# A hybrid decoder step: softmax steps, mixed norm and samples' output set in other slots

## The reference

```python
xn = rms_norm(x, norm1_g); proj = xn @ w_in                     # 2048 -> 5128 columns
y_pool, y_conv = causal_pool_mix(...), h_b * causal_dwconv(h_c * h_x, ...)   # 512 wide each
y_att = attn_fn(q, k, v, logf)                                  # 8 heads of 128
mix = concatenate([rms_norm(y_pool), rms_norm(y_conv), rms_norm(y_att)])     # 512, 512, 1024 wide
x = x + mix @ w_o
xn2 = rms_norm(x, norm2_g); a, gate = split(xn2 @ w_up, 2)
x = x + (silu(causal_dwconv(a, ...) + ffn_conv_b) * gate) @ w_down
```

## Time and profile before

| what | value |
|---|---|
| median of 3 runs | 2859.94 us (2858.17 to 2873.46) |
| the profiled execution, its own time | 2860.91 us |
| its span (first to last instruction) | 2859.3 us |
| PE busy | 2640.5 us, 92% |
| PE in the chain that ended last | 77% |
| DMA in that chain | 11% |
| slots 2 to 80 | about 100 to 611 us |
| mixers, heads | 611 to 716 us, 716 to 998 us |
| mixed norm up to chunk 2 of the output projection | 998 to 1050 us |
| output projection | up to 1276 us |
| second norm and first feed-forward tiles | 1276 to 1323 us |

### The profile page before, as it was taken

The page is one execution under the profiler, slowest core; times in us unless marked ns, Lnnn a source line. Parts: engine busy times, 40 slices in busy tenths (PEclk is TensorE's granted clock), DMA queues, the critical chain, the costliest instruction groups (busy, mean ns, idle before and its releaser), DMA issues.

```text
span 2859.3 us, 50522 instructions
## 1 busy us (share of the span) xinstructions
PE 2640.5 (92%) x19656; PEld 2322.7 (81%) x19656; DVE 1429.8 (50%) x5629; ACT 730.8 (26%) x979; POOL 149.5 (5%) x305
## 2 busy tenths in 40 slices
PE   5899999987677779989999999999999999999998
PEld 3799889862233246668999999999999999999998
DVE  4787766766788442235343443434343434343433
ACT  4332222222333241223222222222222222222221
POOL 0100000013111112100000000000000000000000
PEclk8999999989777789988999999999999999999999
DMA  7689999998999867724222322222222232222221
GB/s 240 243 286 339 324 338 333 337 341 314 391 384 366 323 238 261 250 94 148 89 89 95 101 100 90 89 89 89 89 89 89 95 101 100 89 89 89 89 89 64
DMA packets 274531, 532.94 MB, mean 186 GB/s; under 512 B 16410, under 2 KB 177787, under 8 KB 272980
## 3 DMA queue, kind: packets, MB, share of 16 engines
q1 hardware_dynamic: 216301, 367.81, 37.1%
q0 software_dynamic: 37744, 136.17, 12.9%
q10 hardware_dynamic: 20247, 25.73, 2.5%
HBM read 503.94 MB, written 24.05 MB: 185 GB/s over the span
## 4 chain that ended last, share of the span: by engine, by line
PE 77%; DMA 11%; DVE 6%; issue 2%; ACT 1%; SPq 1%; POOLq 0%; ACTq 0%; POOL 0%; DVEq 0%
PE ps L708 77%; DMA t_r<-in_cache_k 8%; DVE t_work L1786 4%; DMA t_r<-in_cache_v 2%; DMA t_wraw<-in_w_in 1%; PE ps L711 1%; ACT t_wh L1228 0%; DVE t_wl L1623 0%; SPq L582 0%; DMA t_wraw<-in_w_o 0%; DVE t_nmax L1924 0%; DVE t_work L1623 0%; SPq L568 0%; DVE t_auxL L1931 0%; DVE t_xl L1623 0%
## 5 line engine op out<-in xcount | busy, mean ns | idle before, releaser
L708 PE MATMUL ps<-t_xh,t_wh 128*128 128x260 f32 (+1 forms) x4352 | 950.1, 294 | 11.2 <-DVE t_xl L1623 11.1
L708 PE MATMUL ps<-t_xh,t_wl 128*128 128x260 f32 (+1 forms) x4352 | 937.3, 291 | 0.0
L708 PE MATMUL ps<-t_xl,t_wh 128*128 128x260 f32 (+1 forms) x4352 | 935.8, 291 | 0.0
L1623 DVE TENSOR_TENSOR t_wl<-t_wraw,t_wh 128x1024 fp32r<-128x1024 f32 x376 | 460.2, 1225 | 896.1 <-ACT t_wh L1228 896.0
L1228 ACT ACTIVATE t_wh<-t_wraw 128x1024 fp32r<-128x1024 f32 x376 | 398.0, 1060 | 1648.6 <-PE ps L708 1648.4
L708 PEld LDWEIGHTS ps<-t_xh,t_wh 128*128 128x128 f32 x4352 | 686.7, 190 | 86.7 <-issue 60.5
L708 PEld LDWEIGHTS ps<-t_xh,t_wl 128*128 128x128 f32 x4352 | 686.8, 190 | 11.8
L708 PEld LDWEIGHTS ps<-t_xl,t_wh 128*128 128x128 f32 x4352 | 686.2, 190 | 9.4
L1786 DVE CUSTOM_DVE_ANT_0 t_work<-t_r,t_work 128x128 f32<-128x128 f32 x2048 | 455.2, 288 | 130.7 <-DMA t_r<-in_cache_k 119.8
L708 PE MATMUL ps<-t_hh,t_wh 128*128 128x260 f32 x1408 | 285.7, 284 | 3.4 <-issue 3.4
L708 PE MATMUL ps<-t_hh,t_wl 128*128 128x260 f32 x1408 | 284.6, 284 | 0.0
(11 more groups left out here) (256 smaller groups left out, 1187.0 us busy)
## 6 DMA issues: line engine op xcount, KB each, us to landing
t_r<-in_cache_k SPq DMA_DIRECT2D x256, 512.0 KB, 7.7
t_r<-in_cache_v POOLq DMA_DIRECT2D x244, 512.0 KB, 6.6
t_wraw<-in_w_up SPq DMA_DIRECT2D x44, 2048.0 KB, 8.0
t_wraw<-in_w_in SPq DMA_DIRECT2D x22, 2048.0 KB, 9.4
t_wraw<-in_w_down SPq DMA_DIRECT2D x22, 2048.0 KB, 7.8
t_wraw<-in_w_o SPq DMA_DIRECT2D x11, 2048.0 KB, 8.7
scr_proj<-t_stg ACTq DMA_DIRECT2D x40, 256.0 KB, 4.9
t_aux<-scr_proj ACTq DMA_DIRECT2D x8, 768.0 KB, 17.4
```

The source lines that it names most:

```text
L708: return pe.matmul(out, lhsT, rhs, start=start, stop=stop)
L1623: return dve.tensor_tensor(out, in0, in1, op)
```

## The change

Four things are edited.

1. **The relay's distances.** PE's three steps move from `K_END` + 1, 2, 4 to + 2, 4, 7; DVE's from + 1, 2, 3, 4, 5 to + 1, 3, 5, 6, 8; ACT's exponentials from + 3 to + 5. The first value page may come at + 6 instead of + 4. The table `VALUES` has after it, in every slot from 22 to 172, one pair of pages less done than before; the last pair is in slot 173 (before: 172).
2. **Half of the mixed norm beside head 7.** The totals of groups 0 and 1, their rstd and tiles 0 to 7 stand in slots 142 to 147 (`EARLY` = 142) with the stages of head 7; totals go through bank 5 of PSUM one after the other. The samples' share of these groups (`sample_squares`, `sample_sums`) moves too, its Ln and Exp on ACT to slot 148.
3. **The output projection begins at slot 150** instead of 152, and there are 182 slots instead of 184. Group 2 and tiles 8 to 15 remain in slots 149 and 150, with the heads and rests of the first four weight chunks between them.
4. **`sample_out_attention(8)` and `(10)`** stand ahead of `norm(1)` instead of behind the first step of the first feed-forward tile.

```diff
     at = 0
     for r in range(DEC):
-        at = max(at, k_end[r] + 4)
+        at = max(at, k_end[r] + 6)
...
 KEYS, VALUES, K_END, V_END = page_slots()
-OUT0 = TAIL + 3
+EARLY = TAIL - HSTEP
+OUT0 = TAIL + 1
...
 V_LAST = {s: r for r, s in enumerate(V_END)}
-MISC = sorted({s + d for s in K_END for d in (1, 2, 4)} | {s + 1 for s in V_END})
+MISC = sorted({s + d for s in K_END for d in (2, 4, 7)} | {s + 1 for s in V_END})
...
+        TOTALS = (5, 5, 2)
...
@@ -874,14 +876,14 @@
                     return
                 if MISC_N[s] > 1:
                     pe.wait_ge(m_read, MISC_N[s] - 1)
-                if s - 1 in K_LAST:
-                    pe.wait_ge(c_mx, K_LAST[s - 1] + 1)
+                if s - 2 in K_LAST:
+                    pe.wait_ge(c_mx, K_LAST[s - 2] + 1)
                     last = tr(ps[0:HEADS, 7, 0:P], mx8[:, :], P)
-                if s - 2 in K_LAST:
-                    pe.wait_ge(c_dg, K_LAST[s - 2] + 1)
+                if s - 4 in K_LAST:
+                    pe.wait_ge(c_dg, K_LAST[s - 4] + 1)
                     last = mm(ps[:, 7, P:P + HEADS], ones[0:HEADS, :], diag[:, :])
-                if s - 4 in K_LAST:
-                    pe.wait_ge(c_ps, K_LAST[s - 4] + 1)
+                if s - 7 in K_LAST:
+                    pe.wait_ge(c_ps, K_LAST[s - 7] + 1)
                     last = mm(ps[:, 7, 136:144], ones[:, :], ps8[:, :])
...
-                    mm(ps[:, g, :], ones[:, :], msum[g]).then_inc(x_tot, 1)
+                    if g == 1:
+                        pe.wait_ge(x_log, 1)
+                    mm(ps[:, TOTALS[g], :], ones[:, :], msum[g]).then_inc(x_tot, 1)
...
+                if s in (EARLY, EARLY + 2):
+                    mix_totals(((s - EARLY) // 2,))
+                if s == EARLY + 4:
+                    pe.wait_ge(x_log, 2)
+                    pe.wait_ge(y_norm, Y_SQ)
+                    mm(ps[:, 5, 0:64], ones[:, :], sqS[:, 0:64]).then_inc(y_norm, 1)
                 if s == TAIL:
-                    mix_totals((0, 1))
-                    pe.wait_ge(y_norm, Y_SQ)
                     pe.wait_ge(h_rowsC, 2 * HEADS)
-                    mm(ps[:, 3, 0:64], ones[:, :], sqS[:, 0:64]).then_inc(y_norm, 1)
-                if s == TAIL + 1:
                     mix_totals((2,))
                 if s == LAST + 2:
                     pe.wait_ge(y_norm, YA_SQ)
@@ -1104,21 +1110,20 @@
                     head(*at_head)
                 misc(s)
 
+            pe.wait_ge(y_norm, YA_N)
+            pe.wait_ge(ws_kept, 8)
+            pe.wait_ge(w_loaded[1], 16 * (R_O // 2 + 6))
+            sample_out_attention(8, lambda k, c: wraw[:, 1, 2048 * k + 512 * c:2048 * k + 512 * (c + 1)])
+            for i in range(RING):
+                pe.wait_ge(v_loaded[i], 16 * (V_LOADS[i] + 1))
+            sample_out_attention(10, lambda k, c: vring[:, 2 * k + c // 2, 512 * (c % 2):512 * (c % 2 + 1)])\
+                .then_inc(y_norm, 1)
             norm(1)
...
                 def between(u, kt):
-                    if (u, kt) == (0, 1):
-                        pe.wait_ge(y_norm, YA_N)
-                        pe.wait_ge(ws_kept, 8)
-                        pe.wait_ge(w_loaded[1], 16 * (R_O // 2 + 6))
-                        sample_out_attention(8, lambda k, c: wraw[:, 1, 2048 * k + 512 * c:2048 * k + 512 * (c + 1)])
-                        for i in range(RING):
-                            pe.wait_ge(v_loaded[i], 16 * (V_LOADS[i] + 1))
-                        sample_out_attention(10, lambda k, c: vring[:, 2 * k + c // 2, 512 * (c % 2):512 * (c % 2 + 1)])\
-                            .then_inc(y_norm, 1)
...
-                    act.activation(msum[g], ps[:, g, :], ACT.Ln, bias=epsc[:, :],
+                    act.activation(msum[g], ps[:, TOTALS[g], :], ACT.Ln, bias=epsc[:, :],
...
-                if s == TAIL:
-                    act.wait_ge(h_done, HEADS)
-                    mix_square(15, 15)
-                    mix_rstds((0, 1))
-                if s == TAIL + 1:
-                    mix_rstds((2,))
-                if s == TAIL:
-                    for n in range(2):
-                        for b in range(2):
-                            act.wait_ge(h_stored[n][b], 16 * 4)
-                if TAIL <= s < TAIL + 2:
-                    head(0, CHUNKS + 2 * (s - TAIL))
-                    head(0, CHUNKS + 2 * (s - TAIL) + 1)
-                if s == TAIL + 1:
+                if s in (EARLY + 1, EARLY + 3):
+                    mix_rstds(((s - EARLY) // 2,))
+                if EARLY + 2 <= s < EARLY + 6:
+                    if s == EARLY + 2:
+                        for n in range(2):
+                            act.wait_ge(h_stored[n][0], 16 * 4)
+                    for t in (2 * (s - EARLY - 2), 2 * (s - EARLY - 2) + 1):
+                        mix_head(t)
+                if s == EARLY + 6:
                     act.wait_ge(y_norm, Y_RED)
                     act.activation(rsS[:, 0:2, :], rsS[:, 0:2, :], ACT.Ln, bias=epsc[:, :], scale=1.0 / 512).then_inc(y_norm, 1)
                     act.wait_ge(y_norm, Y_LOG)
                     act.activation(rsS[:, 0:2, :], rsS[:, 0:2, :], ACT.Exp, scale=-0.5).then_inc(y_norm, 1)
-                if TAIL + 1 <= s < TAIL + 5:
-                    for t in range(4 * (s - TAIL - 1), 4 * (s - TAIL)):
+                if s == TAIL:
+                    act.wait_ge(h_done, HEADS)
+                    act.wait_ge(x_lo, 8)
+                    mix_square(15, 15)
+                    head(0, CHUNKS)
+                    mix_rstds((2,))
+                    head(0, CHUNKS + 1)
+                    for n in range(2):
+                        act.wait_ge(h_stored[n][1], 16 * 4)
+                if s == TAIL + 1:
+                    for t in range(8, 12):
                         mix_head(t)
+                    head(0, CHUNKS + 2)
+                    for t in range(12, 16):
+                        mix_head(t)
...
-                if s - 3 in K_LAST:
-                    r = K_LAST[s - 3]
+                if s - 5 in K_LAST:
+                    r = K_LAST[s - 5]
                     act.wait_ge(c_sub, r + 1)
                     probs = Eb[:, r * PAGES:(r + 1) * PAGES, :]
...
-                if s - 2 in K_LAST:
+                if s - 3 in K_LAST:
                     last = dve.tensor_reduce(mx1[:, :], ps[0:HEADS, 7, 0:P], AX.X, ALU.max)
-                if s - 3 in K_LAST:
-                    r = K_LAST[s - 3]
-                    last = dve.tensor_copy(maxall[:, r:r + 1, :], ps[:, 7:8, P:P + HEADS])
                 if s - 5 in K_LAST:
                     r = K_LAST[s - 5]
+                    last = dve.tensor_copy(maxall[:, r:r + 1, :], ps[:, 7:8, P:P + HEADS])
+                if s - 8 in K_LAST:
+                    r = K_LAST[s - 8]
...
-                if s - 2 in K_LAST:
+                if s - 3 in K_LAST:
                     dve.tensor_scalar(diag[:, :], ident[0:HEADS, 0:HEADS], mx1[:, :], None, ALU.mult).then_inc(c_dg, 1)
-                if s - 3 in K_LAST:
-                    r = K_LAST[s - 3]
+                if s - 5 in K_LAST:
+                    r = K_LAST[s - 5]
...
-                if s - 4 in K_LAST:
-                    r = K_LAST[s - 4]
+                if s - 6 in K_LAST:
+                    r = K_LAST[s - 6]
...
+            def mix_pair(t):
+                dve.wait_ge(x_sum, 15 if t < 8 else 16)
+                mix_norm(t)
+                mix_norm(t + 1)
+                mix_rest(t)
+                mix_rest(t + 1)
...
-                    last = dve.tensor_reduce(rsS[:, g, :], ps[:, 3, lo * DEC:hi * DEC].rearrange("p (k b) -> p b k", b=DEC),
+                    last = dve.tensor_reduce(rsS[:, g, :], ps[:, 5 if g < 2 else 3, lo * DEC:hi * DEC].rearrange("p (k b) -> p b k", b=DEC),
...
+                if s == EARLY + 1:
+                    sample_squares(0, 8)
+                if EARLY + 2 <= s < EARLY + 6:
+                    mix_pair(2 * (s - EARLY - 2))
+                if s == EARLY + 5:
+                    sample_sums(0, 2, Y_TOT)
                 if s == TAIL:
                     mix_sum(15, 2)
-                    sample_squares(0, 8)
-                if TAIL <= s < TAIL + 2:
-                    if s == TAIL:
-                        dve.wait_ge(h_O, HEADS)
-                    weight_rest(0, CHUNKS + 2 * (s - TAIL))
-                    weight_rest(0, CHUNKS + 2 * (s - TAIL) + 1)
+                    dve.wait_ge(h_O, HEADS)
+                    weight_rest(0, CHUNKS)
+                    weight_rest(0, CHUNKS + 1)
+                    sample_scale(0, 2, Y_RS)
                 if s == TAIL + 1:
-                    sample_sums(0, 2, Y_TOT)
-                if s == TAIL + 2:
-                    sample_scale(0, 2, Y_RS)
-                if TAIL + 1 <= s < TAIL + 5:
-                    for t in (4 * (s - TAIL - 1), 4 * (s - TAIL - 1) + 2):
-                        mix_norm(t)
-                        mix_norm(t + 1)
-                        mix_rest(t)
```

(9 more changed lines are left out.)

1 line of the change is left out of this document (added).

## The result

The changed kernel took 2849.78 us (median of 8 runs, 2841.90 to 2854.64); the kernel before, on the same chip between these runs, 2868.21 us. The ratio is 0.9940, 95% interval 0.9916 to 0.9964: 17.2 us faster (10.3 to 24.1), where 30.8 were forecast. The direction was right, the size was not, and 2849.78 lies just above the range. That it lies next to the 2851 of the first two rivals together confirms neither of them: part of it is a slower base, the next paragraph.

A forecast was written before the change was run, and what follows sets the result against it. PE was taken as the bound nearly everywhere, key pages in the heads. From the profiled 2860.9 us, -14.5 - 1.0 - 11.6 + 0.3 - 4.0 = -30.8 gave 2830.1, as a median 2829; range 2818 to 2849.

The forecast's parts named there:

- the first two rivals: Pages come late anyway in the input projection, and the moved norm gives nothing at head 7; together 2851 us, chance 0.07.
- the three places where it is idle: Ends of four sequences in the input projection, passage from last head into output projection, second norm; edits pay only there.
- the value pair: Input projection: the value table does one pair less by slot 80, -1.0 us there; it reappears in the output projection.
- arrives at 421.2: Input projection, sequence end: one slot more brings PE 0.6 us after it needs `mx8`; 14.5 of 16.0 us gained.
- The first rival: Input projection: without PE's stalls DVE falls behind until PE waits for pages; gives back 11 us, 2840; chance 0.14.
- the 17.6 at the mark: Output projection: PE is through chunk 1 and the first `sample_out` at 1032.1 instead of 1049.7; net -11.6 us after owed work.
- The start of head 7: PE's work fits into its 6.24 us wait, one pair stands elsewhere: -2.9, total of group 1 gives back 1.1.
- The hold behind it: Head 7: ACT's norm work holds DVE, maxima 4 us late, the probabilities' transposition at about 1000, 6.7 us late.
- the second rival: The moved norm gives nothing: head 7's delay is 15 us and not 7, 2840 us; chance 0.10.
- The owed 6.0: Output projection: 4.2 us of value pages and 1.8 us of small matmuls still to do after the earlier mark.
- The slower side: Rival: in-order DVE and ACT hold head 7 until `xl` is full later than 1061 us, kernel slower; chance 0.05.
- The loads' drain: Rival: by the skill page's drain, four table loads in head 7's chain cost 5.5 us more, 2835; chance 0.04.

The follow-up runs named there:

- x_wlate: The changed kernel with SP issuing each slot's 2 MB weight load behind that slot's key pages instead of ahead; ratio to the kernel before 0.9888 (-32.1 us).

## Why the prediction was wrong, point by point

**What bounds the kernel.** PE as the bound and the three places where it is idle: right. What I passed over was in the earlier trace rows: I read DVE's 7.69 us for a key page as a circumstance of the stall and not as its cause, and never added up DVE's waits for pages: 79.4 us from 100 to 606 us, and 42.8 more for ACT, that is at PE's pace.

**Edit 1 (-15.5 with the value pair; measured -9.8).** The step that failed is "with one slot more between, PE multiplies a chunk of 48 matmuls (5.7 us) and arrives at 421.2". It took PE's readiness at 415.43 from a trace in which PE had been held at the two sequence ends before. Without those it arrives earlier: 416.92 is 421.13 less 4.2 us already won. DVE's time for `mx8` (419.88 + 0.61 before, 419.42 + 0.61 after) is set by key pages in SP's program and stayed. So PE waited three times for `mx8`, 8.8 us, where I had said that no such wait would be left. So each stall removed makes the next one likelier, up to DVE's pace, and one slot does not buy the same at all four ends. The argument that there was "DMA for it" counted bytes at the heads' 377 GB/s. It was right that the bytes fit, and said nothing of their order: the stretch stayed at 324 GB/s, and only the loads' place brought 339. The first rival, pages late anyway, had the cause right and its price too high: it gave back 5.7 of 15.5 (1.4 to 10.0 by the interval of edit 1), not 11.

**Edits 2 and 3 (-11.6; measured -7.2, between 2.6 and 11.8).** The second step that failed is "Before, PE idles 10.44 us ahead of 1024.87", all of which I took off for these edits in the 17.6 at the mark. The idle time is gone in the changed kernel, but it takes both parts of the change: with edit 1 alone 5.1 us of it are left, by its later table, and with edits 2 and 3 alone 4.1 us. Compared with kernels of the same table, the stretch from head 6 to the first `sample_out` is shorter by 9.4 us (89.1 against 98.5, old table) and 9.1 (84.0 against 93.1, later one), not by 17.6.

The start of head 7 was mis-sized too. The copy of the key rows was to come 1.8 us earlier, since PE's work would fit into a wait of 6.24 us for value pages. In the trace after it comes 41.3 us after head 6's transposition (994.40 - 953.13) against 37.3 before (986.34 - 949.01), 3.9 late. PE waits there for value pages too, 2.77 and 1.66 us, and its other work went at a granted clock of 0.57 from 974 to 994 us (0.70 from 966 to 986 before); the total of group 1 takes 1.9. But one trace says little: the six with edits 2 and 3 and ACT's old order have 32.3 to 41.3, mean 36.6, the seven without 34.4 to 37.4, mean 36.3. What is shown is that nothing was gained there.

The hold behind it was right: forecast 8.5 us more (from 984.5 to 1000, before 6.9), measured 8.0 (1009.33 - 994.40 = 14.9 against 993.27 - 986.34 = 6.9), and the same within 0.9 in all six traces. Together head 7 is 11.9 us longer in the trace after, between my 6.7 and the second rival's 15, and over the 10 us that I had named as a sign of being wrong. From there to the first `sample_out` it took 32.0 us, forecast 31; but that holds with the later table only, with the old one it is 38.4 and 38.7. The owed 6.0 hold: after leads by 7.4 us at the first `sample_out` (1041.32 against 1048.67) and by 1.1 at the end of the output projection. By the traces edits 2 and 3 would then be worth 3.1 to 3.4 us, by the times 7.2, within whose interval that lies.

**Edit 4 (-4.0; measured -5.2, between 0.6 and 9.8).** As forecast in its steps; the size is known to a few us only: the sum at full clock, 1.12 us; no wait for the weight rows of (14); the two calls inside PE's idle time. From the end of the output projection (1275.55 before, where PE's idle time began, and 1274.48 after, where the first of the two calls begins) to the last step it is 38.3 and 33.5 us: -4.8.

**The base.** Some 8 us of the 21 between forecast and result are the median: three runs with a median of 2859.94 (one of them at 2873.46) and a profile of 2860.91 stood for a kernel whose median over 8 to 35 runs is 2866 to 2869. That is bad luck and not mechanism; without it the result would lie inside the range, and the effects would be as far off.

**The slower side.** Head 7's hold never came near 31 us. The loads' drain did not show.

## What to carry to other kernels

A wait of PE for a vector engine is to be followed to what that engine waited for itself, and the waits summed over the stretch. Where an in-order engine lost 5 to 9 us at a time on transfers that stand behind a large one in SP's program, moving the consumer a slot later moved the wait, and moving one line of that program was worth 22 us, by the points more than the whole change (17). The line's own waits belong to it: what stands behind them is not issued. When a stall is taken away, forward the arrival times through all the later ones; they were recorded with the engine already held. An idle time is not to be credited to one edit before it is known whether another takes part of it. And an in-order engine that gets work between the steps of a critical chain had it better ahead of the instruction on which it waited anyway than behind: 5 to 8 us of hold less in head 7.

## What the runs showed of the hardware

The order of a 2 MB load, with the wait ahead of it, and two pages of 512 KB in SP's program changed what the DMA moved over 506 us from 324 to 339 GB/s, and DVE's waits for pages from 119.1 to 39.9 us. A page issued 1.7 us after such a load landed 13.4 us after its issue, the median key page around it 5.9. For two loads in the heads the same move gave nothing that can be measured (0.9868 and 0.9866).

A stall of PE cost about 1.2 times its idle time: between the first and the fourth sequence's end the changed kernel takes 318.3 us (210.00 to 528.27), x_wlate 306.3 (199.85 to 506.16), 12.0 us more for 10.0 us of waits (8.8 for `mx8`, 1.2 for `t_ocomb`); x_wlate has no wait of PE there. It is one pair of traces.

Executions of the kernel before spread by 0.7% on each chip (2858.42 to 2877.88 us in 35 on one, 2854.55 to 2874.27 in 23 on another), more than most effects measured here. A comparison of two traces gave -6.5 us for a change that is worth 17.
